# Hybrid decoder layer on one core: the cross-attention's value and output products joined into one matrix, formed during self-attention

## The reference, cut to what matters

```python
mn = rmsnorm(mem, mem_norm)
q = (hn @ w_xq).reshape(B, S, X_HEADS, X_HEAD_DIM)
kv = (mn @ w_mem_kv).reshape(B, M, 2, X_HEADS, X_HEAD_DIM)
k, v = kv[:, :, 0], kv[:, :, 1]
s = jnp.einsum('bshd,bmhd->bhsm', q, k) * X_HEAD_DIM ** -0.5
p = jax.nn.softmax(s, axis=-1)
o = jnp.einsum('bhsm,bmhd->bshd', p, v).reshape(B, S, D_MODEL)
return o @ w_xo
```

## Time and profile before

| what | value |
|---|---|
| runs of the kernel, median (lowest to highest of 3) | 2778.23 us (2775.17 to 2782.41) |
| profiled execution, its time | 2782.9 us |
| profiled execution, its span, first to last instruction | 2781.1 us |
| PE busy in the span | 96% |
| granted TensorE clock, mean | 0.988 of 2.4 GHz |
| memory stage on PE | 8 to 71 us |
| self-attention (B) | 370 to 673 us |
| output projection (C) | 673 to 793 us |
| cross-attention (X) | 793 to 1110 us |
| experts | from about 1180 us to the end |

### The profile page before, as it was taken

The page is one execution under the profiler, slowest core; times in us unless marked ns, Lnnn a source line. Parts: engine busy times, 40 slices in busy tenths (PEclk is TensorE's granted clock), DMA queues, the critical chain, the costliest instruction groups (busy, mean ns, idle before and its releaser), DMA issues. The chain is left out here.

```text
span 2781.1 us, 53131 instructions
## 1 busy us (share of the span) xinstructions
PE 2667.9 (96%) x19145; PEld 2280.5 (82%) x19146; DVE 1087.5 (39%) x2664; ACT 629.2 (23%) x1385; POOL 377.9 (14%) x390
## 2 busy tenths in 40 slices
PE   8999998888999999799999999999999999999997
PEld 5445456655477876799999999999999999999997
DVE  1111146553221222442334344344445454545454
ACT  0233345553011211011111111111212121121213
POOL 0000022221000000011111111111111111212112
PEclk9999999999999999799999999999999999999999
DMA  7111242123200000855666677787888888888885
GB/s 285 40 52 53 66 136 67 47 68 115 85 1 9 30 30 38 313 192 198 225 211 245 240 264 269 264 277 267 301 297 307 297 305 288 303 293 307 286 294 197
DMA packets 100329, 525.57 MB, mean 189 GB/s; under 512 B 23954, under 2 KB 50514, under 8 KB 75680
## 3 DMA queue, kind: packets, MB, share of 16 engines
q1 hardware_dynamic: 79488, 490.60, 48.1%
q0 software_dynamic: 20768, 33.97, 5.7%
HBM read 502.44 MB, written 56.33 MB: 201 GB/s over the span
## 5 line engine op out<-in xcount | busy, mean ns | idle before, releaser
L1243 PE MATMUL bank<-xe_t,slot 128*128 128x128 f32 (+4 forms) x8192 | 1025.7, 287 | 13.8 <-issue 12.6
L1243 PEld LDWEIGHTS bank<-xe_t,slot 128*128 128x128 f32 x8192 | 1016.3, 192 | 16.2 <-issue 16.0
L1650 PE MATMUL wide<-act_t,slot 128*128 128x128 f32 (+4 forms) x4096 | 513.2, 286 | 0.0
L1650 PEld LDWEIGHTS wide<-act_t,slot 128*128 128x128 f32 x4096 | 506.3, 191 | 0.0
L2151 DVE TENSOR_SCALAR glu<-bank,b_gu 128x256 f32<-128x256 f32 x256 | 123.9, 484 | 752.8 <-PE bank L1243 752.8
L1190 ACT ACTIVATE sig<-glu 128x256 f32<-128x256 f32 x256 | 106.6, 417 | 851.8 <-DVE glu L2151 849.4
L1295 PE MATMUL bank<-w_in,xt 128*128 128x512 f32 (+1 forms) x512 | 218.7, 581 | 3.8 <-DVEq L1794 3.8
L1201 ACT ACTIVATE y_t<-wide,b_dn 128x256 f32<-128x256 f32 x256 | 107.3, 470 | 427.4 <-PE wide L1650 427.4
L872 POOL DMA_INDIRECT xg<-d_xn,gidx x66 | 66.0, 999 | 904.6 <-DVEq L2110 894.6
L1295 PEld LDWEIGHTS bank<-w_in,xt 128*128 128x128 f32 x512 | 96.0, 193 | 104.5 <-issue 104.5
L885 POOL DMA_INDIRECT share<-d_gate,sidx x64 | 67.6, 1056 | 459.4 <-DVEq L2170 435.7
(11 more groups left out here) (280 smaller groups left out, 2309.8 us busy)
## 6 DMA issues: line engine op xcount, KB each, us to landing
slot<-in_w_gu SPq DMA_DIRECT2D x128, 2048.0 KB, 7.9
slot<-in_w_dn SPq DMA_DIRECT2D x64, 2048.0 KB, 7.7
w_in<-in_w_in SPq DMA_DIRECT2D x1, 6144.0 KB, 26.3
w_mem_k<-in_w_mem_kv SPq DMA_DIRECT2D x4, 1024.0 KB, 11.0
w_mem_v<-in_w_mem_kv SPq DMA_DIRECT2D x1, 4096.0 KB, 19.8
x_sb<-in_x SPq DMA_DIRECT2D x8, 512.0 KB, 3.3
cneg<-d_cneg SPq DMA_DIRECT2D x8, 512.0 KB, 6.6
w_o<-in_w_o SPq DMA_DIRECT2D x1, 4096.0 KB, 18.1
```

Source lines behind the costliest of these rows:

```text
L1243: m = pe.matmul(dst, l, r_, start=(k == 0), stop=(k == n - 1))
L1650: x = pe.matmul(pp2[b][:, (m % 2) * CAP:(m % 2) * CAP + w], slots[4 + m // 4][:, k, (m % 4) * P:(m % 4 + 1) * P], act_t[:, k, 0:w], start= ...
```

## The change

The values of the memory are kept transposed (`vm_t`). During B, 8 products for each head pair form a 256-column slice of (values times `w_xo`), for each cross head and each half of the 256 memory tokens, into `pp[1]`; ACT copies each head's bank (128 by 512) to `mix_out`, SP stores it to a scratch in DRAM (`d_vw`), and C loads the 4 MB back as `vw` in place of `w_xo`. X then multiplies `px_t` by `vw` at once: its products with `vm`, their two ACT copies and `x_ox` go. In B, rounds 7 to 14 each begin with one such product, of two chunks, ahead of `turned(p)` (and behind `scores_pair` where that comes first). The values of rounds 7 to 15 all use bank `pp[0]`; bank `pp[1]` has rounds 1, 3 and 5 and the 4 mixed heads. `w_o` is loaded and scaled in two parts, 6 and 2 row blocks, since the slice of `w_xo` lies where its last two go; the fourth slice lies elsewhere.

```diff
-        vm = Region(55, 63)("vm", [P, S.MT, D])
+        vm_t = Region(55, 63)("vm_t", [P, KD, S.M])
...
+        MIX = D // HP
+        mix_w = [Region(119, 127)("mix_w", [P, KD, MIX]), Region(63, 71)("mix_w_last", [P, KD, MIX])]
...
+        B_MIX = [(NT - 1 + n, n // S.MT, n % S.MT) for n in range(S.XH * S.MT)]
+        B_VALUES = [1 if p < NT - 1 and p % 2 else 0 for p in range(NP)]
+        B_PO = [B_VALUES.count(0), B_VALUES.count(1) + S.XH]
...
+            def mix_load(h, last=False):
+                if last:
+                    sp.wait_ge(b_v, 2 * HP - 1)
+                load(mix_w[last][:, :, :], rows(a["w_xo"][0])[:, :, bass.ds(h * MIX, MIX)], mix_in)
+
+            def mix_store(h, hd, last=False):
+                s = hd % 2
+                sp.wait_ge(mix_full, mix_full_done + S.XH * h + hd + 1)
+                sp.dma_start(d_vw[hd * S.M:(hd + 1) * S.M, bass.ds(h * MIX, MIX)].rearrange("(u m) n -> m u n", u=S.MT),
+                             mix_out[last][s][:, :, :]).then_inc(mix_free[s], 16)
...
+            def b_loads(h, last_mix):
                 load_mla(h + 1)
+                mix_store(h, 0)
                 spread(h, 0)
+                for hd in range(1, S.XH):
+                    mix_store(h, hd)
                 load_fox(h + 1)
+                mix_load(h + 1, last_mix)
+                if last_mix:
+                    load(w_o[:, W_O_FIRST:, :], rows(a["w_o"][0])[:, W_O_FIRST:, :], ld["w_o"])
                 spread(h, 1)
...
-            load(w_xo[:, :, :], rows(a["w_xo"][0]), ld["w_xo"])
+            for s in range(2):
+                sp.wait_ge(mix_free[s], mix_free_done[s] + 16 * (HP * S.XH // 2 + 1))
+            load(vw[:, :, :], rows(d_vw), ld["w_xo"])
...
+            def mix_evict(h, hd, last):
+                s = hd % 2
+                if last and hd == 0:
+                    ac.wait_ge(b_v, 2 * HP)
+                ac.wait_ge(mix_free[s], mix_free_done[s] + 16 * (S.XH // 2 * h + hd // 2 + 1))
+                ac.wait_ge(b_po[1].full, b_po[1].base + B_PO[1] * h + b_mix_use(hd))
+                apart(ac)
+                ac.activation(mix_out[last][s][:, :, :].rearrange("p u n -> p (u n)"), pp[1][:, :], ACT.Copy)\
+                    .then_inc(b_po[1].free, 1)
+                ac.drain().then_inc(mix_full, 1)
...
                     if p:
                         b_out(h, p - 1)
+                    for at_, hd, mt in B_MIX:
+                        if at_ == p and mt == S.MT - 1:
+                            mix_evict(h, hd, last)
...
-                for g in range(2):
-                    ac.wait_ge(x_pp[g].full, x_pp_use(g, "V", i))
-                    ac.activation(ox_t[:, 4 * g:4 * g + 4, :].rearrange("p k t -> p (k t)"), pp[g][:, :],
-                                  ACT.Copy).then_inc(x_pp[g].free, 1)
-                ac.drain().then_inc(x_ox, 1)
...
+            for g in range(KD // 2):
+                b = n % 2
+                pe.wait_ge(m_pp[b].free, n // 2 + 1)
+                for j in range(2):
+                    c = 2 * g + j
+                    m = product(pp[b][:, j * S.M:(j + 1) * S.M],
+                                [(w_mem_v[:, k, c * P:(c + 1) * P], mem_t[:, k, :]) for k in range(KD)])
...
-                (y, i), b = B_PAIRS[p], p % 2
+                (y, i), (b, use) = B_PAIRS[p], b_values_use(p)
...
+            def mixed(h, hd, mt, last):
+                if mt == 0:
+                    pe.wait_ge(b_po[1].free, b_po[1].base + B_PO[1] * h + b_mix_use(hd))
+                    if hd == 0:
+                        pe.wait_ge(mix_in, mix_in_done + 16 * (h + 1))
+                dc = S.XD // P
+                m = product(pp[1][:, mt * MIX:(mt + 1) * MIX],
+                            [(vm_t[:, hd * dc + c, mt * P:(mt + 1) * P], mix_w[last][:, hd * dc + c, :]) for c in range(dc)])
+                if mt == S.MT - 1:
+                    m.then_inc(b_po[1].full, 1)
...
                     if pair and y == 1 and not turn_first:
                         scores_pair(*nxt)
+                    for at_, hd, mt in B_MIX:
+                        if at_ == p:
+                            mixed(h, hd, mt, last)
...
-                pe.wait_ge(x_ox, i + 1)
+                pe.wait_ge(x_pxt, i + 1)
...
-                            [(ox_t[:, k, :], w_xo[:, k, g * 512:(g + 1) * 512]) for k in range(KD)])\
+                            [(px_t[:, k, :], vw[:, k, g * 512:(g + 1) * 512]) for k in range(KD)])\
...
-                pe.wait_ge(x_pxt, i + 1)
-                for g in range(2):
-                    pe.wait_ge(x_pp[g].free, x_pp_use(g, "V", i))
-                    for j in range(4):
-                        c = 4 * g + j
-                        m = product(pp[g][:, j * P:(j + 1) * P],
-                                    [(vm[:, mt, c * P:(c + 1) * P], px_t[:, (c // dc) * S.MT + mt, :])
-                                     for mt in range(S.MT)])
```

More of the change, by code:

```diff
@@ L407, in build @@
         c_pt = [b_pt[b].after(B_PT[b] * HP) for b in range(2)]
-        c_pp = [b_po[b].after(NP // 2 * HP) for b in range(2)]
+        c_pp = [b_po[b].after(B_PO[b] * HP) for b in range(2)]
         x_pt = [c_pt[b].after(NT // 2) for b in range(2)]
@@ L419, in turn_out_use @@
             return e_pt[b].base + 4 * i + 6 + k
-        e_gu = [x_pp[b].after(2 * NT) for b in range(2)]
+        e_gu = [x_pp[b].after(NT) for b in range(2)]
         a_x = Handoff(sem, "a_x")
@@ L640, in _ @@
             load_fox(0)
-            load(w_o[:, :, :], rows(a["w_o"][0]), ld["w_o"])
-            with sp.Fori(0, HP - 1) as h:
+            mix_load(0)
+            load(w_o[:, 0:W_O_FIRST, :], rows(a["w_o"][0])[:, 0:W_O_FIRST, :], ld["w_o"])
+            def b_loads(h, last_mix):
                 load_mla(h + 1)
+                mix_store(h, 0)
                 spread(h, 0)
+                for hd in range(1, S.XH):
+                    mix_store(h, hd)
                 load_fox(h + 1)
+                mix_load(h + 1, last_mix)
+                if last_mix:
+                    load(w_o[:, W_O_FIRST:, :], rows(a["w_o"][0])[:, W_O_FIRST:, :], ld["w_o"])
                 spread(h, 1)
+            with sp.Fori(0, HP - 2) as h:
+                b_loads(h, False)
+            b_loads(HP - 2, True)
+            mix_store(HP - 1, 0, True)
             spread(HP - 1, 0)
+            for hd in range(1, S.XH):
+                mix_store(HP - 1, hd, True)
             barrier(sp, 3)
@@ L801, in _, with gain @@
                 po.memset(square[y][:, :], 0.0)
+            def gain(k0, k1):
+                for k in range(k0, k1):
+                    po.tensor_tensor(w_o[:, k, :], w_o[:, k, :], g_out[:, k:k + 1].to_broadcast([P, D]), ALU.mult)
+                return po.drain()
             po.wait_ge(ld["w_o"], 16)
[L803 to L805 removed]
+            gain(0, W_O_FIRST)
             with po.Fori(0, HP - 1) as h:
@@ L1269, in _ @@
             pe.wait_ge(ld["w_mem_v"], 16)
-            for t in range(S.MT):
-                for g in range(D // 512):
-                    b = n % 2
-                    pe.wait_ge(m_pp[b].free, n // 2 + 1)
-                    product(pp[b][:, :], [(mem_t[:, k, t * P:(t + 1) * P], w_mem_v[:, k, g * 512:(g + 1) * 512])
-                                          for k in range(KD)]).then_inc(m_pp[b].full, 1)
-                    n += 1
+            for g in range(KD // 2):
[5 more added lines that the diff above has]
+                                [(w_mem_v[:, k, c * P:(c + 1) * P], mem_t[:, k, :]) for k in range(KD)])
+                m.then_inc(m_pp[b].full, 1)
+                n += 1
             barrier(pe, 1)
@@ L1775, in _ @@
                 n += 1
-            for t in range(S.MT):
-                for g in range(D // 512):
-                    b = n % 2
-                    ve.wait_ge(m_pp[b].full, n // 2 + 1)
-                    ve.tensor_copy(vm[:, t, g * 512:(g + 1) * 512], pp[b][:, :]).then_inc(m_pp[b].free, 1)
-                    n += 1
+            for g in range(KD // 2):
+                b = n % 2
+                ve.wait_ge(m_pp[b].full, n // 2 + 1)
+                ve.tensor_copy(vm_t[:, 2 * g:2 * g + 2, :].rearrange("p k t -> p (k t)"), pp[b][:, :])\
+                    .then_inc(m_pp[b].free, 1)
+                n += 1
             barrier(ve, 1)
```

44 lines of the change are left out of this document (28 added, 16 removed).

## The result

The changed kernel is slower by 0.5%: 2794.77 us median of 4 runs (2788.86 to 2797.82) against 2779.72 for the kernel before, ratio 1.0048 (95% interval 1.0035 to 1.006). The forecast was 2775, with a range up to 2787. The profiled execution of the change is its fastest run, 2788.86 us with a span of 2787.1; before it was 2782.9 and 2781.1. So the two traces differ by 6 us where the medians differ by 15: the trace of before is of an execution slower than its median, that of the change of one faster.

The account below looks back on a forecast made before the run. PE was taken to bound X, a PE-DVE-ACT chain to pace B. -32.4 + 28.4 + 0.5 = -3.5 us (profiled 2782.9 to 2779.4), or 2775 on the median's footing; own range 2768 to 2782, 8 in 10 from 2758 to 2787.

Parts of the forecast that it names:

- X: -32.4: Cross-attention: products with `vm` (29.4 us), two PE waits (2.3) and the last tile's wait (0.72) go, -32.4 us.
- B inside a head pair: Self-attention: PE lateness adds 5.9 us per head pair; the period grows by 7.5, the last by 5.9.
- The waits: Self-attention: PE waits on ACT for the mixed products' bank, 1.6 us once and 1.2 twice a head pair, 16 in all.
- The gaps of rounds 8, 10, 12 and 14: Self-attention: PE's idle gaps in these rounds (1.61, 0.87 and 0.40, 0.61, 0.83 us) absorb work of the mixed products.
- 28.4: Self-attention in all: 23.6 us over four head pairs plus 4.8 for `values(15)`, +28.4 us.
- `values(15)`: 3 times 1.6: Self-attention, round 15: values wait 1.6 us for shared bank `pp[0]` in three head pairs, 4.8 us.
- Memory stage: +0.5: Memory stage: 64 records of 512 columns become 128 of 256, costing +0.5 us, between 0 and 2.3.
- Transfers. ... I cost these at nothing: SP's added slice loads, stores and `vw` load are hidden behind other work: nothing, with up to 3 us in the range.
- ACT's four copies ... cost nothing more: Self-attention: ACT's four copies a head pair stand before exponentials where ACT waits on DVE anyway, so no further cost.
- Rival 2: Self-attention: gaps absorb nothing, each head pair pays 10.9 us; 48.4 in B, +16.5 in all, 2795; chance 0.13.
- Rival 1: Self-attention: the bank never delays PE, 7.2 us in B, `values(15)` free; -24.7 in all, 2753; chance 0.18.

Follow-up runs that it names:

- e2: Changed kernel with ScalarE's four head pairs written out instead of looped, other engines keeping their loops: 2771.7 us, 23.1 us faster than the change.
- g1: Kernel before with ScalarE's four head pairs written out instead of looped, nothing else: 2777.8 us, against 2782.1 for the kernel before beside it.
- f2: Kernel before with 30 bare semaphore increments at the start of ScalarE's program, loop body unchanged: 2791.2 us, 12.7 us slower than the kernel before.
- h1: Changed kernel with 98 bare semaphore increments at the start of ScalarE's program, its loop ending at 515: 12.3 us faster than the change.
- f3: Changed kernel with ScalarE's head pairs written out and the new order of banks and copies: 2755.7 us, 0.86% faster than the kernel before.
- f1: Kernel before with 30 bare semaphore increments inside ScalarE's loop body: 14.5 us slower than the kernel before.
- g4: Changed kernel, loop kept, new bank order, `load_fox` ahead of the last `mix_store` and `mix_w` behind `spread(h, 1)`: 5 us gained over the bank order alone (2775.4).
- e1: Changed kernel with the `mix_w` load (and the rest of `w_o`) issued behind `spread(h, 1)` instead of ahead: 4.3 us faster than the change.
- e3: Changed kernel, mixed banks copied out before the previous round's values, values of round 5 on `pp[0]`, 15 on `pp[1]`: 2775.4 us, 19.4 us faster than the change.
- f4: Changed kernel with 130 bare semaphore increments at the start of ScalarE's program, loop ending at 547: ScalarE idles of 6.31 and 5.94 us; no time given.

## Why the prediction was wrong

- **X: -32.4.** Right. X is 284 us long, with 282.7 of PE, and its first `w_xq` record to the first expert record shrank from 347.1 to 314.9 us: -32.2.
- **B inside a head pair: 5.9 or, with `values(15)`, 7.5.** Right within about 1 us. Without the stalls (e2) the period is 81.9: +6.5 against before, +7.3 against g1, which has the same edit to ACT's loop. The last pair is +7.0 against g1, for 5.9. The waits came where and as long as forecast: 1.7 at round 7 for 1.6, 1.3 at rounds 11 and 13 for 1.2, together 16.8 us for 16. The gaps of rounds 8, 10, 12 and 14 took the products. B of e2 is 25.2 us longer than before and 27.8 longer than that of g1, for 28.4.
- **`values(15)`: 3 times 1.6.** 1.87 each in the change, 5.6 us in all.
- **Memory stage: +0.5.** The 128 records take 27.8 us (before: 27.6), so nothing was lost. B began 1.7 us earlier, because the key products ended earlier; I have no cause for that, and f2, with the memory stage of the kernel before, moved by 1.5.
- **The step that failed: "Transfers. ... I cost these at nothing".** I had looked at each transfer's landing against its reader, and there the cover held: POOL's wait for `rr_all` grew from 3.32 to 8.5 and 9.7 us, hidden. What I left out is that SP's queue is not the only user of the DMA engines. ScalarE's own instructions come that way, and I had counted ACT's four copies a head pair as free, since they stand where ACT waits anyway. The 28 instructions they bring moved the end of ACT's loop from 387 to 417, past an edge at which the way back needs a fetch. "ACT's four copies ... cost nothing more" is the second half of the same error. Its price is some 15 to 17 us of B where the sum had 0, an estimate: the 19.7 between the change and e2, less what the loop costs without a stall (2.6 by g1, 4.7 by the longer waits of h1).
- **Rival 2**, "the gaps don't absorb anything", gives 2795, the measured time to 0.2 us. It is wrong all the same: its sign, waits ahead of the transposes of rounds 10, 12 and 14 as long as before, is absent. That a rival's number is met says nothing for its mechanism.
- **Rival 1**, a bank that never holds PE up, gave 2753. f3 comes near it (2755.7), once the banks are ordered for it and the fetch is gone; its B is +10.5, or +13.1 against g1, where the rival had +7.2, and PE still waits 4.1 us for `mix_out`.

Without the stall, in e2, the parts are -0.3 ahead of B, +25.2 in B, -1.4 in the output projection, -32.8 in X and -1.9 in the experts: -11.2, and its span is 11.3 shorter than that of before. The forecast was -3.5; 3.2 of the difference is B, and 3.3 lies in the output projection and the experts, where f2 differs from before by 5.0 with the same code. Against g1 the parts are +0.6, +27.8, 0, -32.6 and -1.9: -6.1. So B and X, the two terms that make up the forecast, were each right to 0.6 us once both kernels are without the loop; what failed is the term that was put at nothing.

## What to carry to other kernels

Count what an edit adds to the instruction stream of every engine that loops, not only its busy time: 30 instructions that do nothing cost the kernel before 13 us, once a loop's end passed an edge, and writing that one engine's loop out made the changed kernel 23 us faster. Before a transfer is costed at nothing, look at which branches fall in its time: an idle on "issue" at a way back, with more instruction packets on the page, is the sign. And where products are put into gaps, let their bank be emptied ahead of copies that come later anyway: the order of two copies and of two banks was worth 19 us with the loop and 16 without it.

## What the runs showed of the hardware

- ScalarE's stall at the way back is 2.66 to 2.74 us with nearly idle DMA queues (f2, and f1's first end), 2.7 to 3.0 with 2 MB of loads issued some 7 to 9 us ahead of the way back (g4), 3.4 to 3.6 with 2 MB just ahead (e1), 5.9 to 6.3 with 3 MB (change, e3, f4). f1's second end, where loads begin in the middle of the stall, has 4.23.
- A loop of 248 or 276 instructions without this stall fetches nothing while it runs (no packet of q14 from 450 to 600 us before, none from 460 to 610 in h1); with it, five packets of 8 KB come each time round.
- It comes by the place of the loop's end in the engine's program, with an edge between an end at 402 and at 417, and again between 517 and 547. What is held at that moment, and from where it is counted, was not measured.
- PE's clock falls around such a stall and outlasts it. In f2 a wait of 2.6 us is followed by a stretch at 0.50, the lower level, 1.2 GHz; B grew by 9.6 us for two such waits, 5.1 us together. In the change the fall had begun before ACT stalled, behind the wait of 1.87 us at `values(15)`, in whose stretch the clock reads 0.66; at the third end, with the same wait, it reads 1.00. A wait of PE in a stage that otherwise keeps it busy can so cost nearly twice its length (9.6 for 5.1), or only its length.
